# A hybrid decoder step: a scan's input copied out of PSUM by ScalarE, side work put later in its slot, and decode batches begun at other slots

## The reference, cut to what matters

```
xn = rmsnorm(x, g_mix_norm);  z = xn @ w_in              # 2048 -> 5120, split in q k v u h gb gc
o  = attend(q, k, v)       # prompt: masked attention over 256 tokens
                           # sample: each batch against 2048 cached keys and values, three dilated windows
x_re, x_im = u @ b_re, u @ b_im                          # state-space layer, 32 groups of 64 complex states
h[t] = a * h[t-1] + x[t]                                 # complex, decaying and turning; a scan over time
y  = gelu(Re(c * h) + d * u);  y = y * sigmoid(y @ w_glu + b_glu)
yc = gb * conv3(gc * h_in)
x  = x + concat(rmsnorm(o), rmsnorm(y), rmsnorm(yc)) @ w_out
x  = x + (silu(xn2 @ w_gate) * (xn2 @ w_up)) @ w_down    # 2048 -> 5632 -> 2048
y  = rmsnorm(x, g_final)
```

## Time and profile before

| | |
|---|---|
| runs | median 1616.28 us of 3 (1615.83 to 1616.48) |
| the profiled execution | 1614.72 us, span 1612.9 us, mean granted TensorE clock 0.981 |
| PE busy | 1524.2 us (94%) |
| VectorE, ScalarE, POOL busy | 814.8 (51%), 559.7 (35%), 239.4 (15%) |
| DMA | 296.59 MB, mean 184 GB/s |
| chain that ended last | PE 79%, DVE 8%, DMA 5%, POOL 3%, ACT 3%, issue 2% |

### The profile page before, as it was taken

One profiled execution on the slowest core, in us unless ns is written; L12 is line 12 of the kernel. 1 busy time (PEld: TensorE's weight loads), 2 busy tenths in 40 slices (PEclk: granted clock), 3 DMA queues, 4 the chain that ended last, 5 costly groups with the idle time before them and its releaser, 6 DMA issues.

```text
span 1612.9 us, 26917 instructions
## 1 busy us (share of the span) xinstructions
PE 1524.2 (94%) x11064; PEld 1431.2 (89%) x11064; DVE 814.8 (51%) x1038; ACT 559.7 (35%) x732; POOL 239.4 (15%) x368
## 2 busy tenths in 40 slices
PE   9989788889998999999999999999999899999995
PEld 9978666666766789999999999999999899999995
DVE  6668776564336657744444444444444333333434
ACT  6322122223545434443333333333333223333333
POOL 7795434220043000000000000000000000000101
PEclk9999899999999999999999999999999999999998
DMA  7653587878777775444444444444444344544442
GB/s 253 189 197 110 202 321 288 322 294 318 293 263 284 271 105 163 147 153 146 150 149 149 150 147 152 145 154 144 154 144 152 112 153 145 157 143 157 145 154 82
DMA packets 80530, 296.59 MB, mean 184 GB/s; under 512 B 13376, under 2 KB 14016, under 8 KB 74944
## 3 DMA queue, kind: packets, MB, share of 16 engines
q1 hardware_dynamic: 80448, 295.42, 55.4%
HBM read 289.31 MB, written 5.43 MB: 183 GB/s over the span
## 4 chain that ended last, share of the span: by engine, by line
PE 79%; DVE 8%; DMA 5%; POOL 3%; ACT 3%; issue 2%; DVEq 0%; ACTq 0%; SPq 0%; POOLq 0%
PE ps L1757 19%; PE ps L1758 19%; PE ps L1759 19%; PE ps L1664 5%; PE ps L1666 4%; PE ps L1665 4%; DMA vt<-in_cv 4%; PE ps L1496 2%; DVE wlo L854 2%; PE ps L1471 2%; ACT whi L565 1%; DMA raw<-in_w_out 1%; PE ps L1710 1%; PE ps L1712 1%; PE ps L1711 1%
## 5 line engine op out<-in xcount | busy, mean ns | idle before, releaser
L1112 DVE TENSOR_TENSOR wlo<-raw,whi 128x1024 fp32r<-128x1024 f32 x264 | 325.0, 1231 | 523.0 <-ACT whi L745 522.8
L745 ACT ACTIVATE whi<-raw 128x1024 fp32r<-128x1024 f32 x264 | 279.8, 1060 | 613.3 <-PE ps L1759 608.8
L1758 PE MATMUL ps<-xl,whi 128*128 128x320 f32 x1400 | 432.7, 309 | 0.0
L1757 PE MATMUL ps<-xh,whi 128*128 128x320 f32 x1400 | 432.7, 309 | 0.0
L1759 PE MATMUL ps<-xh,wlo 128*128 128x320 f32 x1400 | 432.7, 309 | 0.0
L1664 PE MATMUL ps<-xh,whi 128*128 128x320 f32 x768 | 254.3, 331 | 17.5 <-DVE wlo L854 8.8
L1759 PEld LDWEIGHTS ps<-xh,wlo 128*128 128x128 f32 x1400 | 262.8, 188 | 0.0
L1758 PEld LDWEIGHTS ps<-xl,whi 128*128 128x128 f32 x1400 | 262.8, 188 | 0.0
L1757 PEld LDWEIGHTS ps<-xh,whi 128*128 128x128 f32 x1400 | 262.8, 188 | 0.0
L1665 PE MATMUL ps<-xl,whi 128*128 128x320 f32 x768 | 242.1, 315 | 0.0
L1666 PE MATMUL ps<-xh,wlo 128*128 128x320 f32 x768 | 242.0, 315 | 0.0
(11 more groups left out here) (276 smaller groups left out, 1445.0 us busy)
## 6 DMA issues: line engine op xcount, KB each, us to landing
raw<-in_w_gu SPq DMA_DIRECT2D x176, 512.0 KB, 3.5
raw<-in_w_dn SPq DMA_DIRECT2D x88, 512.0 KB, 3.5
raw<-in_w_in SPq DMA_DIRECT2D x80, 512.0 KB, 5.1
kt<-in_ck SPq DMA_DIRECT2D x40, 1024.0 KB, 5.9
vt<-in_cv SPq DMA_DIRECT2D x80, 512.0 KB, 7.1
raw<-in_w_out SPq DMA_DIRECT2D x32, 512.0 KB, 4.5
x<-in_xt SPq DMA_DIRECT2D x8, 320.0 KB, 8.3
out_kv<-z SPq DMA_DIRECT2D x2, 1280.0 KB, 9.5
```

Source lines behind the costliest of these rows:

```text
L745: act.activation(whi[:, j % SPL, :], raw[:, j % RAW, :], ACT.Copy).then_inc(S["w_hi"], 1)
L1112: v.tensor_tensor(wlo[:, j % SPL, :], raw[:, j % RAW, :], whi[:, j % SPL, :].bitcast(F32), ALU.subtract) \
L1757: t_.matmul(out, whi[:, slot, w], ah[:, k, :], start=(k == 0), stop=False)
L1758: t_.matmul(out, whi[:, slot, w], al[:, k, :], start=False, stop=False)
```

## The change

It has these parts:
- Batches start at slots 37, 43, 50, 56, 63, 69, 76 and 81. SAMPLE_SLOT goes from 92 to 93, and the block of the decode outputs is spread over SAMPLE_SLOT (VectorE scales, ScalarE squares), + 1 (ScalarE's high part) and + 2 (VectorE's low part and sums).
- `project(i)` is one slot earlier. ScalarE copies banks 6 and 7 into a new tile `xs` (semaphore `x_moved`), before its `high(s + 2)`; VectorE's rotation reads `xs`. The banks are released by `x_moved`. The copy waits for the rotation of the tile before.
- The scan over 640 columns is two over 320, and `dec` is 320 wide, made by a tensor_scalar.
- At a slot's end PE now does the decode batches first, then the prompt: output of pair r two slots after its scores, turned probabilities (from the middle) and values in the slot between. ScalarE's copies follow that order. `po` and `vs` keep bank 5.
- VectorE: norms of the prompt at the beginning of the second slot in place of the end of the first; `mask_scores` before `low(s + 2)` in place of behind.
- POOL makes |a|^2 and clears `qst` first; VectorE's reciprocal is in slot 2.
- SP: the prompt's mask waits for `dec_ready`, and two groups of x are reloaded a slot later.

```diff
-START_OF = (37, 43, 49, 55, 61, 67, 73, 79)
-SAMPLE_SLOT = START_OF[-1] + 13
+START_OF = (37, 43, 50, 56, 63, 69, 76, 81)
+SAMPLE_SLOT = START_OF[-1] + 12
...
-        dec = scan_place.take("dec", [P, 2, NT])
+        dec = scan_place.take("dec", [P, NT])
+        xs = scan_place.take("xs", [P, 2, NT])
...
+        def projected(s):
+            return [i for i in range(ST) if scan_slot(i, 0) - 1 == s]
...
-                    "x": lambda: ("x_rot", key[1] + 1),
+                    "x": lambda: ("x_moved", key[1] + 1),
...
-                if s == PROMPT0 + 16:
+                if s == PROMPT0 + 17:
                     sy.wait_ge(S["po_done"], NF)
...
-                for r in prompt_pair(s, 1):
-                    prompt_probabilities(r)
+                for i in projected(s):
+                    act.wait_ge(S["x_proj"], i + 1)
+                    if i:
+                        act.wait_ge(S["x_rot"], i)
+                    act.activation(xs[:], ps[:, 6:8, 0:NT], ACT.Copy).then_inc(S["x_moved"], 1)
...
+                for r in prompt_pair(s - 2, 0):
+                    act.wait_ge(S["po_done"], r + 1)
+                    act.activation(z[:, ZQ + r, 0:SEQ], ps[:, 5, 0:SEQ], ACT.Copy).then_inc(S["po_moved"], 1)
+                for r in prompt_pair(s, 1):
+                    prompt_probabilities(r)
+                    act.wait_ge(S["vs_done"], r + 1)
+                    act.activation(vs[:].rearrange("p a n -> p (a n)"), ps[:, 5, 0:2 * P], ACT.Copy).then_inc(S["vs_moved"], 1)
...
-                    dve.wait_ge(S["x_proj"], i + 1)
-                    step(v.tensor_tensor(tm[:, 0:2], ps[:, 6:8, 0:NT], c_, ALU.mult), wait=False)
-                    v.tensor_tensor(tm[:, 2:4], ps[:, 6:8, 0:NT], s_, ALU.mult).then_inc(S["x_rot"], 1)
+                    dve.wait_ge(S["x_moved"], i + 1)
+                    step(v.tensor_tensor(tm[:, 0:2], xs[:], c_, ALU.mult), wait=False)
+                    v.tensor_tensor(tm[:, 2:4], xs[:], s_, ALU.mult).then_inc(S["x_rot"], 1)
...
+                for r in prompt_pair(s, 1):
+                    prompt_norms(r)
...
+                for step_ in range(KN):
+                    for b in batches(s, step_):
+                        mask_scores(b, step_)
                 low(s + 2)
-                for r in prompt_pair(s, 0):
-                    prompt_norms(r)
...
-                if s == 10:
+                if s == 2:
                     dve.wait_ge(S["den_ready"], 1)
-                    v.reciprocal(par[:, 4, :], par[:, 3, :]).then_inc(S["den_turned"], 1)
+                    v.reciprocal(par[:, 10, :], par[:, 10, :]).then_inc(S["den_turned"], 1)
...
-                g_.tensor_tensor(dec[:], keep_m[:].rearrange("p (a n) -> p a n", a=1).to_broadcast([P, 2, NT]),
-                                 decay[:, i:i + 1].rearrange("p (a n) -> p a n", a=1).to_broadcast([P, 2, NT]), ALU.mult).then_inc(S["dec_ready"], 1)
+                g_.tensor_scalar(dec[:], keep_m[:], decay[:, i:i + 1], None, ALU.mult).then_inc(S["dec_ready"], 1)
...
+                for r in prompt_pair(s - 2, 0):
+                    prompt_output(r)
+                for r in prompt_pair(s, 1):
+                    turn_prompt(r)
                     prompt_values(r)
```

More of the change, by code:

```diff
@@ L1057, in _ @@
                     v.tensor_tensor(sqa[:, 0, sample], sqa[:, 1, sample], sqa[:, 0, sample], ALU.add).then_inc(S["sq_added"], 1)
-                for step_ in range(KN):
-                    for b in batches(s, step_):
-                        mask_scores(b, step_)
                 for b in batches(s, 5):
@@ L1242, in _ @@
             pool.wait_ge(S["vec_in"], 16)
+            step(g_.tensor_tensor(arr(9), are, are, ALU.mult), wait=False)
+            step(g_.tensor_tensor(arr(10), aim, aim, ALU.mult))
+            g_.tensor_tensor(arr(10), arr(9), arr(10), ALU.add).then_inc(S["den_ready"], 1)
+            g_.memset(qst[:], 0.0).then_inc(S["q_zero"], 1)
             DT, MAG, ANG = 0, 1, 2
@@ L1591, in end @@
             def end(s):
-                for r in prompt_pair(s, 0):
+                for b in batches(s, 11):
+                    if b >= LATE:
+                        turn_output(b)
+                for b in batches(s, 6):
+                    turn_probabilities(b, 2)
+                for b in batches(s, 5):
+                    turn_probabilities(b, 0)
+                    turn_probabilities(b, 1)
+                for step in range(KN):
+                    for b in batches(s, step):
+                        scores(b, step)
+                for step in range(6, 11):
+                    for b in batches(s, step):
+                        values(b, 2 * step - 12)
+                        values(b, 2 * step - 11)
+                for r in prompt_pair(s - 2, 0):
+                    prompt_output(r)
+                for r in prompt_pair(s, 1):
+                    turn_prompt(r)
                     prompt_values(r)
-                for r in prompt_pair(s, 1):
-                    prompt_output(r)
                 if s == BT_SLOT:
@@ L1611, in end @@
                         last.then_inc(S["vn_done"], 1)
-                for b in batches(s, 11):
-                    if b >= LATE:
-                        turn_output(b)
-                for b in batches(s, 6):
-                    turn_probabilities(b, 2)
-                for b in batches(s, 5):
-                    turn_probabilities(b, 0)
-                    turn_probabilities(b, 1)
-                for step in range(KN):
-                    for b in batches(s, step):
-                        scores(b, step)
-                for step in range(6, 11):
-                    for b in batches(s, step):
-                        values(b, 2 * step - 12)
-                        values(b, 2 * step - 11)
                 for b in range(LATE):
```

62 lines of the change are left out of this document (23 added, 39 removed).

## The result

The changed kernel takes **1603.63 us** (median of 7 runs, 1601.54 to 1609.92), the kernel before 1616.48 in the same round: ratio 0.9929, 95% interval 0.9912 to 0.9947. It is 0.7% faster, 12.8 us, where 23.4 were forecast; its lower bound 1577 and upper 1610 hold it, the forecast's own 1586 to 1600 does not. The profiled execution took 1607.65 us, span 1605.8.

The account below looks back on a forecast made before the run. PE was taken as the bound, busy 417.6 of 473.2 us in the four touched stages. Terms summed to -23.4, giving 1591.3 us for an execution like the profiled one and 1593 for the median; range 1577 to 1610.

Parts of the forecast that it names:

- -6.5 for POOL's constants: Before the first rotation: an earlier reciprocal and POOL table let VectorE start at once, saving 6.5 us (bounds -8, -2).
- so I take its own 6.5: First rotation: VectorE set the pace, so its 6.49 us wait for POOL's table was counted as 6.5 saved.
- -19 and +3 for the projection and the copy: Scores' waits on rotations go: -9 in 162.7 to 209.0, -10 in 209 to 384.4 us; value-tile DMA waits grow +3.
- +2 for rotations on two SBUF tensors: Scan rotations: reading two SBUF tensors costs VectorE time, mostly where it has room; +2 us (bounds -4, +12).
- 0.82 to 1.25: Sign to check: the mean time of the first rotation operation's successor was to lie between these values, in us.
- The mechanism named ahead: Rotations meet POOL's table pieces under the exclusive port lock; as a rival, 1632 us, chance 0.08.
- -10 for the prompt: Prompt's probabilities turned at the slot's end and norms first remove 9.1 us idle; -10 us (bounds -12, -5).
- +2.5 for its hand-overs: Prompt's bank hand-overs at slots 68, 74, 80, 81 and 87, about 0.5 each; +2.5 us (bounds +1, +5).
- Masks ahead of the low split, costed at nothing: VectorE's slots: masks first delay the split some 0.5 us under slack; zero, or 3 in all without slack.
- +6 for slots 81 and 82: Batches 6 and 7 five slots apart leave PE 5.1 us idle, then half clock; +6 us (bounds +2, +8).
- -1.4 for the end: Before the first attention unit: 3.0 us idle for al replaces 4.0, with less half clock; -1.4 (bounds -5, +1).
- DMA becomes the bound: Rival, slots 43 to 66: every rotation wait becomes a value-tile wait, losing a -10; 1603 us, chance 0.14.

Follow-up runs that it names:

- e1: Changed kernel with VectorE's reciprocal of POOL's sum back in slot 10 instead of slot 2; 1605.9 us.
- e7: Changed kernel with POOL waiting for VectorE's scales before its products of B; 1604.6 us.
- e6: Changed kernel without the copy xs: projection back in its slot, VectorE rotating out of PSUM; 1612.22 us.
- e9: Changed kernel with only the first five scan tiles projected in their own slot and rotated out of PSUM, without the copy xs; 1596.54 us.
- e14: Changed kernel with batch 6 at slot 75 and the score masks behind VectorE's low split and rotations again, prompt in its new order; 1605.74 us.
- e2: Changed kernel with batch 6 starting at slot 75 instead of 76; 1594.05 us.
- e8: Changed kernel with ScalarE's square of the conv branch moved behind the copies of the probabilities in slot 82; 1602.71 us.
- e3: Changed kernel with VectorE's whole norm chain for the scan branch moved from the end of slot 77 to the end of slot 78; 1601.7 us.
- e4: Changed kernel with all batch start slots of the kernel before; 1596.37 us.
- e5: Changed kernel with batch 6 at slot 75, and the prompt's order and the masks' place of the kernel before; 1600.71 us.
- e10: Changed kernel with batch 6 at slot 75 and VectorE's norm chain cut up between the ends of slots 77 and 78; 1587.98 us.
- e13: Changed kernel with batch 6 at slot 75 and the prompt's order of before, masks still ahead of the low split; 1588.9 us.

## Why the prediction was wrong

The direction was right and the forecast 10.6 us too good. By its own steps, minus is faster:

1. **-6.5 for POOL's constants: about -2, not told from nothing.** The table's wait went, as said. VectorE did start at once: its first rotation comes 2.7 us after the start of slot 24, not 9.2. The step that failed is "so I take its own 6.5": POOL's idle of 7.06 us was cover for VectorE's scales and splits, and I did not ask what POOL, once awake, runs beside. The slot before 12 got 3.3 of wait (e1, e7). And of PE's three large waits in slots 24 to 32 only the first went (3.97 before slot 26); the next grew, from 2.68 to 3.27 for the low split and from 2.76 to 3.95 at 140.
2. **-19 and +3 for the projection and the copy: right after slot 37.** 16.9 by e6's windows for the 16 forecast, and the value tiles' waits grew by 5.9 (forecast 3, bound 8).
3. **+2 for rotations on two SBUF tensors: some +7, with the copy's own part in it.** VectorE's time grew by 7.7 us in all (814.8 to 822.5, inside +2 to +10; the rotations 6.6 and the scans 4.1 more, the turning back 9.1 less), and the mean of 1.02 lies inside 0.82 to 1.25. Mis-sized is where it falls: I put it "mostly where it has room", but five of 16 tiles lie in slots 24 to 37, which VectorE paces (e9: 7.1 us, which holds the copy and the projection's place too). The mechanism named ahead holds: beside these rotations POOL works on its tables, and one of each pair is held. The Trainium skill's exclusive lock ("SBUF — State Buffer", section "SBUF: two separate sides") foretells the direction; by it the scales at slot 12 are the same case, 1.26 beside POOL and 0.49 with POOL still.
4. **-10 for the prompt, +2.5 for its hand-overs: +5. This is the step that failed most.** The term took the 9.1 us for norms queued behind masks and splits, and cured them by a later turn. They were masks behind low splits, not the turn's place. Moving the turn cures nothing (10.9 with it in e14), and moving the norms into the second slot put them behind the norm chain of slot 77, a wait of 5.25 that I had not looked for: the queue ahead of a moved step was read in slots 81 and 82, not in 77 and 78.
5. **Masks ahead of the low split, costed at nothing: -11.7.** I asked only what the split behind them loses (0.5 each), not who waits for the mask: projections, scores and turns, all through banks 6 and 7. Points 4 and 5 come to -6.6 together, where -7.5 was forecast for the first alone: the sum hides both faults.
6. **+6 for slots 81 and 82: +9.6** (e2). The idle in slot 82 was 5.1 as worked out, 3.75 of it at the place named. Mis-sized: slot 81's hand-over at 0.5, measured 2.14, since the copy stands behind exponents and a split on ScalarE; and the half clock, for which I took 1.6 once.
7. **-1.4 for the end: -0.7.** 3.07 and 0.83 of idle for 3.96 and 0.63, read from two traces; half clock follows in both (granted 0.72 over 6.1 us, 0.68 over 5.3), so it brought nothing.

By the runs these are -2 - 8.6 (points 2 and 3, by e6) + 5.1 - 11.7 + 9.6 - 0.7 = -8.3, where -12.8 was measured. Each is a difference of medians good to about 2 us, and the parts lean on one another (the masks bring 5.5 alone, 11.7 in company), so the 4.5 between stay open. That the gain came as near to the forecast as it did is luck: the masks paid for what the prompt and the table lost. Of the rivals, "DMA becomes the bound" gave 1603, but for a reason that did not happen: slots 43 to 67 got 12.1 us shorter.

## What to carry to other kernels

Before a wait is put down to the place of the waiting step, name the instruction that ends it and try moving that one first: here three lines ahead of a split were worth more than a reordered prompt on three engines. An engine's idle time can be cover for its neighbour, so a step that ends it has to be laid against what the neighbour runs then. And where a step moves by one slot, read the queues of every slot it passes through, not only of those where tables meet.

## What the hardware showed

**The same wait is paid once or several times.** The changed kernel and e8 run the same program up to slot 82. In both PE waits 3.27 us for the low split before slot 28:

```profile
118.76 0.42 PE L1668 MATMUL ps<-xh,whi 128*128 128x320 f32 x1 [3.27 <-DVE wlo L860]
```
```profile
118.69 0.64 PE L1668 MATMUL ps<-xh,whi 128*128 128x320 f32 x1 [3.27 <-DVE wlo L860]
```

Yet the window from 111 to 131 us has a granted clock of 1.00 and 109 matmuls in the one, 0.74 and 85 in the other, in the same 16.73 us of busy PE:

```profile
111.00:131.00 20.00, 16.73 (x109) 14.38 (x108) 19.45 (x25) 5.21 (x6) 14.24 (x12) 1.00 0.70 261
```
```profile
111.00:131.00 20.00, 16.73 (x85) 15.28 (x84) 15.77 (x19) 3.88 (x4) 11.82 (x10) 0.74 0.62 237
```

So one execution loses some 5 us (20 x 0.26) behind a wait that costs another nothing more. It isn't these two alone: up to slot 36 the changed kernel, e2, e3, e4, e5, e8, e10, e13 and e14 are one program, and from the end of slot 27 to that of slot 36 their nine traces take 49.5 to 50.0 us four times (granted 0.90 to 0.97) and 52.6 to 53.6 five times (0.84 to 0.87). That fits the spread of 8 us between executions, and it means that a stage of one trace against the same stage of another is good to no better than 4 us where such waits stand. A sum that adds a fixed half clock to each wait is right at best in the mean.

**POOL's `dec` is short alone and long beside VectorE's pair.** Seven of its 16 records are not held, and take 1.08 us for 320 columns as a tensor_scalar, where the tensor_tensor over 640 took 1.25, seven times too: half the columns saved 0.17 us. The other nine take 2.1 to 2.7. In the kernel before, `dec` mostly came in after the first multiply of the pair that turns the scan back, and the second was held (1.87 and 1.89 in the earlier trace rows). Now, in seven of the nine, it starts 0.06 us behind the first, both multiplies run at 0.82, and `dec` takes 2.36, about its own 1.08 and what is left of the two. The wait changed sides, to the engine that has time. Whether the kind of operation or its width did that isn't shown.

```profile
193.72 1.08 POOL L1375 TENSOR_SCALAR dec<-keep_m,decay 128x320 f32<-128x320 f32 x1 [3.78 <-DVE tm L920]
...
210.06 0.82 DVE L923 TENSOR_TENSOR tm<-tm,tab 128x640 f32<-128x640 f32 x1
210.80 0.82 DVE L924 TENSOR_TENSOR tm<-tm,tab 128x640 f32<-128x640 f32 x1
210.12 2.36 POOL L1375 TENSOR_SCALAR dec<-keep_m,decay 128x320 f32<-128x320 f32 x1 [1.50 <-DVE tm L920]
```

**VectorE did not gain on its scans:** 0.92 + 0.86 for the two halves, 1.52 for the whole in the kernel before:

```profile
L913 DVE TENSOR_TENSOR_SCAN tm<-dec,tm 128x640 f32<-128x640 f32 x16 | 24.3, 1520 | 0.3
```
